# Ring slots of split weights at eight different places within 512 bytes

## The reference

```python
h = rms_norm(x, ln_pre_mix)
proj = h @ w_in                       # 2048 x (2048 gMLP + 1536 q,k,v + 4096 gates)
y_a = gmlp_branch(u, v_sg, ...) @ w_a_out
y_b = swa_branch(q, k, v, rel_bias, sinks) @ w_b_out
mix = (gate_a * y_a + gate_b * y_b) @ w_o
x = x + rms_norm(mix, ln_post_mix)
h2 = rms_norm(x, ln_pre_ffn)
x = x + rms_norm(conv_ffn(h2, w_up, conv_w, w_down), ln_post_ffn)
```

## Time and profile before

| what | value |
| --- | --- |
| median of 3 runs | 1596.75 us (1596.64 to 1596.88) |
| profiled execution, first to last instruction | 1595.2 us |
| difference of the median to that span | 1.55 us |
| PE busy | 1585.3 us, 99% of the span |
| DVE busy / ACT busy | 1260.5 us (79%) / 829.2 us (52%) |
| matmuls, and weight loads | 8652 each |
| moved by DMA | 313.15 MB, 196 GB/s |

### The profile page before, as it was taken

How to read it: one execution, slowest core, us unless ns; L and a number is a source line. 1 busy time by engine, 2 the same in 40 slices (tenths; PEclk the granted TensorE clock), 3 DMA queues, 4 the chain that set the end, 5 groups by cost and what they waited for, 6 DMA issues and landing times.

```text
span 1595.2 us, 24342 instructions
## 1 busy us (share of the span) xinstructions
PE 1585.3 (99%) x8652; PEld 1372.3 (86%) x8652; DVE 1260.5 (79%) x1836; ACT 829.2 (52%) x1124; POOL 2.0 (0%) x12
## 2 busy tenths in 40 slices
PE   9999999999999999999999999999999999999998
PEld 7888888888888888888888888888888888888886
DVE  6556677677797787777777777877778899989998
ACT  6544544456565654444444444444444575766664
POOL 0000000000000000000000000000000000000000
PEclk9999999999999999999999999999999999999999
DMA  9895455556566465656555565655656555555552
GB/s 373 265 225 191 159 184 166 177 159 206 193 239 218 149 210 184 189 184 201 188 184 186 184 197 189 191 184 184 194 187 197 198 207 207 205 196 201 184 211 106
DMA packets 234946, 313.15 MB, mean 196 GB/s; under 512 B 5360, under 2 KB 209808, under 8 KB 234000
## 3 DMA queue, kind: packets, MB, share of 16 engines
q1 hardware_dynamic: 231056, 306.44, 58.1%
q10 hardware_dynamic: 3840, 6.05, 1.5%
HBM read 309.58 MB, written 2.88 MB: 196 GB/s over the span
## 4 chain that ended last, share of the span: by engine, by line
PE 99%; DMA 0%; DVE 0%; ACT 0%; issue 0%; SPq 0%; DVEq 0%
PE ps L1502 44%; PE ps L1506 23%; PE ps L1593 18%; PE ps L1786 7%; PE ps L1643 3%; PE ps L1606 1%; PE ps L1517 1%; PE ps L1522 0%; PE ps L1732 0%; PE ps L1713 0%; DMA raw<-in_w_in_dram 0%; PE ps L1725 0%; PE ps L1742 0%; PE ps L1840 0%; DVE arena L1478 0%; PE ps L1546 0%
## 5 line engine op out<-in xcount | busy, mean ns | idle before, releaser
L1502 PE MATMUL ps<-actT,w_hi 128*128 128x512 f32 x3072 | 717.1, 390 | 0.0
L463 ACT ACTIVATE w_hi<-raw 128x1024 fp32r<-128x1024 f32 x420 | 434.2, 1058 | 513.6 <-PE ps L1502 261.1
L870 DVE TENSOR_TENSOR w_lo<-raw,w_hi 128x1024 fp32r<-128x1024 f32 x422 | 506.1, 1222 | 243.3 <-ACT w_hi L463 240.7
L1502 PEld LDWEIGHTS ps<-actT,w_hi 128*128 128x128 f32 x3072 | 569.8, 188 | 114.1 <-issue 0.2
L1506 PEld LDWEIGHTS ps<-actT,w_lo 128*128 128x128 f32 x3072 | 383.4, 191 | 10.0 <-issue 1.7
L1506 PE MATMUL ps<-actT,w_lo 128*128 128x256 f32 x3072 | 389.4, 283 | 0.0
L1593 PE MATMUL ps<-w_hi,xs 128*128 128x512 f32 x832 | 226.8, 389 | 0.0
L1593 PEld LDWEIGHTS ps<-w_hi,xs 128*128 128x128 f32 x832 | 156.1, 188 | 32.6
L1593 PE MATMUL ps<-w_lo,xs 128*128 128x512 f32 x416 | 128.1, 389 | 0.0
L1197 DVE TENSOR_TENSOR w_lo<-raw,w_hi 128x1024 fp32r<-128x1024 f32 x96 | 117.0, 1218 | 0.0
L1387 DVE SCALAR_TENSOR_TENSOR arena<-arena,convw 128x256 f32<-128x256 f32 x256 | 106.7, 479 | 0.0
(11 more groups left out here) (181 smaller groups left out, 933.4 us busy)
## 6 DMA issues: line engine op xcount, KB each, us to landing
raw<-in_w_up_dram SPq DMA_DIRECT2D x128, 1024.0 KB, 5.6
raw<-in_w_down_dram SPq DMA_DIRECT2D x64, 1024.0 KB, 5.3
raw<-in_w_in_dram SPq DMA_DIRECT2D x58, 1024.0 KB, 5.3
raw<-in_w_o_dram SPq DMA_DIRECT2D x16, 1024.0 KB, 5.3
raw<-in_w_a_out_dram SPq DMA_DIRECT2D x8, 1024.0 KB, 5.2
raw<-in_w_b_out_dram SPq DMA_DIRECT2D x8, 1024.0 KB, 5.2
arena<-in_x_dram SPq DMA_DIRECT2D x1, 2048.0 KB, 17.1
arena<-in_x_dram ACTq DMA_DIRECT2D x2, 1024.0 KB, 6.2
```

Source lines behind the costliest of these rows:

```text
L463: act.activation(w_hi[:, h % RING, :], raw[:, h // 2, h % 2 * HALF:(h % 2 + 1) * HALF], ACT.Copy)\
L870: dve.tensor_tensor(w_lo[:, h % RING, :], raw[:, h // 2, h % 2 * HALF:(h % 2 + 1) * HALF], w_hi[:, h % RING, :].bitcast(F32), ALU.subtract ...
L1502: return pe.matmul(ps[:, bank + c, :], w_hi[:, h % RING, at:at + P], actT[:, k, :, :].rearrange("p a s -> p (a s)"), start=start, stop=stop)
```

## The change

The two rings are no longer arrays [128, 4, 1024] but lists of four slices of one array with a pitch of 1152 elements (4608 bytes, nine times 512), each slice shifted by a number of elements of its own. The writers and readers use the same slices as before, with the same sizes, waits and signals. `a_parts` is allocated before `ident` instead of last. The scratch that the program reserves at the bottom of SBUF for DMAs whose descriptors are made by software shrinks from 16384 to 1024 bytes per partition. No such DMA is in the kernel. On every engine the instructions stand in the same order as before, with the same operand shapes.

The places of the operands in the built program, in bytes within 512:

| operand | before | changed |
| --- | --- | --- |
| `w_hi` slots 0, 1, 2, 3 | 128, 128, 128, 128 | 128, 192, 144, 256 |
| `w_lo` slots 0, 1, 2, 3 | 128, 128, 128, 128 | 128, 384, 160, 448 |
| `actT`, `xs`, `raw`, `ident` | 128 | 128 |
| `a_parts` (both parts) | 448 | 128 |
| arena, `rrow`, `stat` | 192 | 192 |

```diff
@@ -92,10 +80,16 @@
 
 
         raw = sb("raw", [P, RAW, UNIT])
-        w_hi = sb("w_hi", [P, RING, HALF], F32R)
-        w_lo = sb("w_lo", [P, RING, HALF], F32R)
+        def ring(name, shifts):
+
+            whole = sb(name, [P, RING * (HALF + P)], F32R)
+            return [whole[:, slot * (HALF + P) + shift:slot * (HALF + P) + shift + HALF] for slot, shift in enumerate(shifts)]
+
+        w_hi = ring("w_hi", (0, 16, 4, 32))
+        w_lo = ring("w_lo", (0, 64, 8, 80))
         actT = sb("actT", [P, KD, 2, S], F32R)
         xs = sb("xs", [P, RING, 2, S], F32R)
+        a_parts = sb("a_parts", [P, 2, 3 * P], F32R)
         ident = sb("ident", [P, P])
         gvec = sb("gvec", [P, 2, KD])
         convw = sb("convw", [P, 3, 2 * FF // P])
@@ -167,7 +161,6 @@
         B1, B2, BT, BLK = 0, 512, 1536, 512
         b_hi, b_lo = forms[:, 0:7 * BLK], forms[:, 7 * BLK:14 * BLK]
         s_hi, s_lo = forms[:, 7168:7680], forms[:, 7680:8192]
-        a_parts = sb("a_parts", [P, 2, 3 * P], F32R)
         a_hi, a_lo = a_parts[:, 0, :], a_parts[:, 1, :]
         s123 = convw[:].rearrange("p i t -> p (i t)")
         s4 = rrow[:, 0:P]
@@ -460,7 +453,7 @@
                     act.wait_ge(raw_landed[h // 2], 16 * m + 16)
                 if not fresh:
                     act.wait_ge(half_used, 8 * m + (h - RING + 1 if free is None else free))
-                act.activation(w_hi[:, h % RING, :], raw[:, h // 2, h % 2 * HALF:(h % 2 + 1) * HALF], ACT.Copy)\
+                act.activation(w_hi[h % RING], raw[:, h // 2, h % 2 * HALF:(h % 2 + 1) * HALF], ACT.Copy)\
                    .then_inc(hi_ready, 1)
 
             def split_xs(m, h, src, free=None):
@@ -520,10 +513,10 @@
 
             for c, ready in enumerate((first_columns_ready, hi_ready)):
                 act.wait_ge(first_half_landed[c], 16)
-                act.activation(w_hi[:, 0, c * 512:(c + 1) * 512], raw[:, 0, c * 512:(c + 1) * 512], ACT.Copy).then_inc(ready, 1)
+                act.activation(w_hi[0][:, c * 512:(c + 1) * 512], raw[:, 0, c * 512:(c + 1) * 512], ACT.Copy).then_inc(ready, 1)
             for c, (landed, ready) in enumerate(((second_half_landed, first_columns_ready), (raw_landed[0], hi_ready))):
                 act.wait_ge(landed, 16)
-                act.activation(w_hi[:, 1, c * 512:(c + 1) * 512], raw[:, 0, HALF + c * 512:HALF + (c + 1) * 512], ACT.Copy)\
+                act.activation(w_hi[1][:, c * 512:(c + 1) * 512], raw[:, 0, HALF + c * 512:HALF + (c + 1) * 512], ACT.Copy)\
                    .then_inc(ready, 1)
             act.wait_ge(small["gains"], 16)
             for h in (2, 3):
@@ -719,7 +712,7 @@
                 act.wait_ge(half_used, unit.free_at(j))
                 act.activation(xs[:, slot, 0, :], unit.sweep.src[:, unit.k + j, :], ACT.Copy)
                 act.wait_ge(raw_landed[unit.slot], unit.landed)
-                act.activation(w_hi[:, slot, :], raw[:, unit.slot, j * HALF:(j + 1) * HALF], ACT.Copy).then_inc(hi_ready, 1)
+                act.activation(w_hi[slot], raw[:, unit.slot, j * HALF:(j + 1) * HALF], ACT.Copy).then_inc(hi_ready, 1)
 
             def middle(sweep):
 
@@ -867,8 +860,8 @@
             def split(m, h):
 
                 dve.wait_ge(hi_ready, 8 * m + (h + 1))
-                dve.tensor_tensor(w_lo[:, h % RING, :], raw[:, h // 2, h % 2 * HALF:(h % 2 + 1) * HALF],
-                                  w_hi[:, h % RING, :].bitcast(F32), ALU.subtract).then_inc(lo_ready, 1)
+                dve.tensor_tensor(w_lo[h % RING], raw[:, h // 2, h % 2 * HALF:(h % 2 + 1) * HALF],
+                                  w_hi[h % RING].bitcast(F32), ALU.subtract).then_inc(lo_ready, 1)
 
             def split_xs(m, h, src):
 
@@ -1224,7 +1217,7 @@
                 slot = (unit.place + j) % RING
                 dve.wait_ge(hi_ready, unit.before + j + 1)
                 rest(xs[:, slot, 1, :], unit.sweep.src[:, unit.k + j, :], xs[:, slot, 0, :])
-                rest(w_lo[:, slot, :], raw[:, unit.slot, j * HALF:(j + 1) * HALF], w_hi[:, slot, :]).then_inc(lo_ready, 1)
+                rest(w_lo[slot], raw[:, unit.slot, j * HALF:(j + 1) * HALF], w_hi[slot]).then_inc(lo_ready, 1)
 
             def middle(sweep):
 
@@ -1499,17 +1492,17 @@
         @block.tensor
         def _(pe):
             def by_hi(h, at, k, c, bank, start, stop):
-                return pe.matmul(ps[:, bank + c, :], w_hi[:, h % RING, at:at + P],
+                return pe.matmul(ps[:, bank + c, :], w_hi[h % RING][:, at:at + P],
                                  actT[:, k, :, :].rearrange("p a s -> p (a s)"), start=start, stop=stop)
 
             def by_lo(h, at, k, c, bank, start, stop):
-                return pe.matmul(ps[:, bank + c, 0:S], w_lo[:, h % RING, at:at + P], actT[:, k, 0, :],
+                return pe.matmul(ps[:, bank + c, 0:S], w_lo[h % RING][:, at:at + P], actT[:, k, 0, :],
                                  start=start, stop=stop)
 
             def half_a(m, h, k0, bank, rows_before):
 
                 early = h < EARLY
-                hi, lo = (early_hi[h], early_lo[h]) if early else (w_hi[:, h % RING, :], w_lo[:, h % RING, :])
+                hi, lo = (early_hi[h], early_lo[h]) if early else (w_hi[h % RING], w_lo[h % RING])
                 pe.wait_ge(hi_ready, 8 * m + (h + 1))
                 for i in range(4):
                     pe.wait_ge(lo_split, rows_before + k0 + i + 1)
@@ -1591,7 +1584,7 @@
                     for xpart, wpart in ((x_hi, w_hi), (x_hi, w_lo), (x_lo, w_hi)):
                         for c in range(2):
                             ins = pe.matmul(ps[:, bank + 2 * t + c, :], xpart[:, tokens],
-                                            wpart[:, slot, c * 512:(c + 1) * 512],
+                                            wpart[slot][:, c * 512:(c + 1) * 512],
                                             start=(first and xpart is x_hi and wpart is w_hi),
                                             stop=(last and xpart is x_lo))
                 ins.then_inc(half_used, 1)
@@ -1604,7 +1597,7 @@
                     for a, wpart in ((0, w_hi), (0, w_lo), (1, w_hi)):
                         for c in columns:
                             ins = pe.matmul(ps[:, 2 * t + c, :], xs[:, slot, a, tokens],
-                                            wpart[:, slot, c * 512:(c + 1) * 512], start=False, stop=(h == 7 and a == 1))
+                                            wpart[slot][:, c * 512:(c + 1) * 512], start=False, stop=(h == 7 and a == 1))
                     return ins
 
                 for h in range(4, 8):
@@ -1917,7 +1910,7 @@
     laid["w_spatial"] = inputs["w_spatial"].transpose(2, 0, 1)
     laid["conv_w"] = inputs["conv_w"].reshape(3, 2 * FF // P, P).transpose(2, 0, 1)
 
-    nc = _bacc.Bacc("TRN2", target_bir_lowering=False, num_devices=1)
+    nc = _bacc.Bacc("TRN2", target_bir_lowering=False, num_devices=1, dynamic_dma_scratch_size=1024)
     arrays, args = {}, []
     for name in _INS + ["bucket_onehot"]:
         a = bucket_onehot() if name == "bucket_onehot" else _np.ascontiguousarray(laid[name])
```

## The result

The changed kernel takes 1612.78 us (median, 1612.67 to 1613.09) against 1596.82 us for the kernel before in the same comparison: ratio 1.0100, 95% interval 1.0088 to 1.0112. It is 16.0 us slower; the forecast was 16.1. The profiled execution has a span of 1610.9 us.

What follows compares the result with a forecast made beforehand. TensorE's matmul pace was taken as the bound. Terms -2.2 + 12.2 + 6.1 + 0 + 0 = +16.1 us on the 1595.2 us span gave 1611.3, plus 1.55 for the median: 1612.8 us, range 1591.5 to 1628.

Steps and rivals of the forecast that it cites:

- What bounds it: Whole kernel: TensorE, busy 99% of the span, sets the time by the pace of successive matmuls; no wait does.
- The price of a moved slot in wide matmuls: L1502: 2304 wide matmuls with stationary weights from moved slots lose 5.3 ns each, +12.2 us.
- Moving weights: L1593, L1606, L1643: 1152 matmuls streaming weights from a moved place lose 5.3 ns each, +6.1 us.
- The sevens: L1786, 24 groups of 21 wide matmuls, six using `a_parts`: moving it to 128 removes their surplus, -2.2 us.
- Narrow matmuls: L1506, 256 columns: 2304 loads from moved slots keep their pace of 119.7 ns, 0 us.
- rival 4: L1506: narrow loads from moved slots lose as wide ones do, +12.2 us, 1625 us; chance 0.12.
- Writers and scratch: ScalarE and VectorE write moved slots as fast as before, and the smaller DMA scratch costs nothing: 0 us.
- Rival 1: Wide matmuls: only stationary place 448 is bad, or none; moved slots cost nothing, 1594.5 to 1596.75 us; chance 0.20.
- Rival 2: Wide runs behind narrow ones: different places separate the reads and remove the switch surplus, -4.7 with the sevens, 1592.0 us; chance 0.15.
- Rival 3: All matmuls: the 13.4 ns over their columns is a clash of equal places; 1518 us, or 1558 at half; chance 0.10.
- The rule weighed against the trace: TensorE's operand reads: by independent ports places can't matter, moved slots cost nothing, the sevens' surplus stays; no change at all.

## Why the prediction was right, point by point

**What bounds it.** Right, and nothing else played a part: TensorE's busy time rose by 16.5 us, the span by 15.7.

**The price of a moved slot in wide matmuls.** The forecast's mechanism was right in this: the distance between the two operands costs. The step took `a_parts` as the nearest row and 5.3 ns from its six matmuls. Slots 1, 2 and 3 of `w_hi` pace at 233.1, 232.2 and 233.3 ns in the up projection, so 5.5 to 6.6 over 226.7. For slot 1 the row was the right one: `a_parts` and slot 1 turned out to be at the same distance, 64 bytes beyond a multiple of 256. That it also served for slots 2 and 3, at 16 and 128 bytes, is luck: the forecast's picture, any difference within 512 bytes, is wrong, since 256 bytes cost nothing and 192 bytes only 1.4 ns. Two things were left out. Slot 0 was to stay at 226.7 and has 231.3, since it is entered from a disturbed state and its eight matmuls aren't enough to settle. And slot 2 stands behind the narrow matmuls, where it had 230.1 already before the change, so that it pays 2.2 ns more and not 5.3. Against before, slots 0, 1, 2 and 3 pay 4.2, 6.5, 2.2 and 6.6 ns over the runs of 32. Together the term is +14.5 us where the sum had +12.2.

**Moving weights.** +6.6 us measured against +6.1. The count of 1152 took in `w_lo` slot 1, which is at 256 bytes, no distance as it turned out, and left out the disturbed ones of slot 0.

**The sevens.** -1.6 us against -2.2. The cause was right, as the version with all shifts 0 shows (4.76 us a seven). That its surplus would go fully was wrong with disturbed matmuls ahead of it. The text doubted whether the nine matmuls behind `a_parts` had the same cause, since they are at 128 themselves. They have: in the trace they go 231 231 236 228 233 231 226 227 226, which ends with the same row of numbers as behind a switch from narrow to wide.

**Narrow matmuls.** This step failed in sign. The sum had 0, and rival 4 gave +12.2 us; measured were -3.6 us. The reason that the text gave for 0, one even pace of 119.7 ns also behind a switch, says nothing of other distances. Nor is 120 ns the lowest pace in the trace of before: behind attention's small matmuls (at 169.3 us) the narrow ones of L1506 go 117 118 117 118 119 121 117 117 before they settle at 120. That was not used.

**The total.** Terms off by +2.3, +0.5, +0.6 and -3.6 us add up to -0.2. That 1612.8 was met to a tenth is the luck of these four; the sign and about the size of the largest two terms were right, and that is what put it in the range. The range's upper end, 1628, is 1 us short of its own bound: 3456 x 10 ns less 2.2 us gives 1629.1.

**Writers and scratch.** 0 and 0, as said: 1222 and 1057 ns a slot, and 1596.92 us with the scratch alone.

**The rivals.** Rival 1 (at most one place, 448, is bad) is refuted by the run with 64 bytes in all `w_hi` slots (233.5 ns). Rival 2 asked for slots at 226.7 or lower behind a switch; none is. Rival 3 put the 13.4 ns over the columns down to equal places; the kernels with one distance show them at distance 0 and more beyond it, and no run got a wide pace below 226.7, so the estimate of 215.8 ns for 512 columns, worked out from the Trainium skill's N / 2.4 + 2.5 ns ("TensorE: Matmul & The Clock Gate", section "Back-to-back issue gap"), was not approached by moving operands. For narrow matmuls a sixth of the surplus could be had (120.4 to 118.1). Rival 4 is wrong, as above.

The rule weighed against the trace was that TensorE has two independent read ports and never waits on anyone (the Trainium skill, "SBUF — State Buffer", section "Who interferes with whom"). What the prediction drew from it, that places can't matter to the time, does not hold: two kernels that differ in 64 bytes of one operand's start differ by 23.9 us (1594.83 and 1618.69). Whether that comes from the ports is not shown by any run.

## What to carry to other kernels

Where TensorE's own pace is the bound, the start addresses of the two operands are part of the kernel: give the stationary and the moving operand of 512-column fp32r matmuls the same place modulo 256 bytes, and look for a tensor that was allocated last and has another. Where only 256 columns stream, 64 bytes between the two did better here (118.1 against 120.4 ns). Before a probe of this kind goes over many slots at once, put one distance everywhere, since a stream that is disturbed in one slot is not settled in the next. And read start-to-start times, not the mean durations of the page: the surplus of 4.7 ns of the changed kernel (227.6 to 232.4) shows there as 390 against 394.

## What the runs showed of the hardware

- The pace depends on the distance between the start addresses of stationary and moving operand, as far as tried modulo 256 bytes; moving both by 64 bytes changes nothing (1594.89 and 1594.83 us), moving some slots by 256 changes nothing (1594.97), and 320 bytes show the two-step pace of 64.
- Wide matmuls (512 columns): 226.7 ns settled at distance 0, 233.3 at 64 (235.8 and 230.8 in turn), 229.0 at 192, and 233.3 at 128 as slot 3 of the changed kernel.
- Narrow matmuls (256 columns) go the other way: 120.0 ns at 0 and 256, 120.0 on average at 128, but 117.8 at 64 and 192.
- At distance 0 a disturbance (a switch from narrow to wide) costs about 27 ns, spread over five matmuls; behind narrow matmuls at 192 or 32 bytes it costs 46 ns over nine.
- What inside TensorE or SBUF does this is not shown by any run, nor are distances below 16 bytes, operands of other types, or one distance alone with the weights moving. Why narrow and wide matmuls prefer different distances stays open.
